# Projecting two of three row chunks first, normalising them beside the third, and leaving the meta rows out after the merge

## What is computed

```python
def _merge(x, o_a, o_b, rb, ga, gb, gla_norm_g, w_pa, w_pb, w_o, g, b):
    ...
    mixed = jax.nn.sigmoid(ga) * y_a + jax.nn.sigmoid(gb) * y_b
    return _layer_norm(ALPHA * x + mixed @ w_o, g, b)

def _ffn(x, w_gate, w_up, w_down, g, b):
    hdn = jax.nn.silu(x @ w_gate) * (x @ w_up)
    return _layer_norm(ALPHA * x + hdn @ w_down, g, b)
```

## Time and profile before

| what | value |
|---|---|
| median of 3 runs | 1925.07 us |
| the profiled execution: its own time, and its span | 1928.97 us, 1927.3 us |
| PE busy, share of the span | 1826.3 us, 95% |
| DVE, ACT, POOL busy | 724.2, 379.4, 475.2 us |
| mean granted TensorE clock | 0.962 |
| merge loop | 711.8 to 987.9 us |
| output projection | 992.4 to 1087.2 us |
| first FFN matmul, first `w_down` matmul | 1122.4, 1178.0 us |
| FFN groups but the last end | 1821.7 us |

### The profile page before, as it was taken

The page is one execution under the profiler, slowest core; times in us unless marked ns, Lnnn a source line. Parts: engine busy times, 40 slices in busy tenths (PEclk is TensorE's granted clock), DMA queues, the critical chain, the costliest instruction groups (busy, mean ns, idle before and its releaser), DMA issues.

```text
span 1927.3 us, 29265 instructions
## 1 busy us (share of the span) xinstructions
PE 1826.3 (95%) x11360; PEld 1654.4 (86%) x11360; DVE 724.2 (38%) x1303; ACT 379.4 (20%) x706; POOL 475.2 (25%) x283
## 2 busy tenths in 40 slices
PE   6999999998989899999999869999999999999994
PEld 5966666665768879999999769999999999999993
DVE  3156767541326352211156643123213313312318
ACT  3132232221312332011110260100100110010032
POOL 3310110110111203322232113322233232332225
PEclk8999999998987979999999989999999999999997
DMA  5134444303551111111111001111111111111102
GB/s 158 47 106 123 117 118 143 95 12 110 171 136 43 36 24 44 44 45 53 44 33 55 23 22 44 45 53 44 44 44 44 44 54 44 39 48 52 46 23 88
DMA packets 166780, 123.19 MB, mean 64 GB/s; under 512 B 22074, under 2 KB 140234, under 8 KB 166706
## 3 DMA queue, kind: packets, MB, share of 16 engines
q1 hardware_dynamic: 163154, 120.94, 21.6%
q10 hardware_dynamic: 3552, 1.25, 0.3%
HBM read 112.31 MB, written 9.85 MB: 63 GB/s over the span
## 4 chain that ended last, share of the span: by engine, by line
PE 88%; DVE 5%; ACT 2%; issue 2%; DMA 1%; SPq 1%; POOL 0%; POOLq 0%; ACTq 0%; DVEq 0%
PE psum L729 16%; PE psum L732 16%; PE psum L733 16%; PE psum L807 4%; PE psum L813 4%; PE psum L811 4%; PE psum L1256 4%; PE psum L1251 4%; PE psum L1255 4%; PE psum L962 4%; PE psum L935 2%; PE psum L938 1%; PE psum L891 1%; PE psum L1012 1%; PE psum L1192 1%
## 5 line engine op out<-in xcount | busy, mean ns | idle before, releaser
L729 PE MATMUL psum<-xh,wh 128*128 128x352 f32 (+1 forms) x1560 | 506.9, 325 | 20.3 <-DVE xl L2236 15.3
L732 PE MATMUL psum<-xl,wh 128*128 128x352 f32 (+1 forms) x1560 | 505.6, 324 | 0.0
L733 PE MATMUL psum<-xh,wl 128*128 128x352 f32 (+1 forms) x1560 | 504.6, 323 | 0.0
L677 POOL CAST wh<-raw 128x1024 fp32r<-128x1024 f32 x126 | 134.1, 1065 | 1406.2 <-PE psum L729 481.6
L729 PEld LDWEIGHTS psum<-xh,wh 128*128 128x128 f32 x1560 | 295.8, 190 | 22.1 <-issue 21.9
L679 POOL TENSOR_TENSOR wl<-raw,wh 128x1024 fp32r<-128x1024 f32 x126 | 310.7, 2466 | 10.1
L732 PEld LDWEIGHTS psum<-xl,wh 128*128 128x128 f32 x1560 | 295.7, 190 | 0.2
L733 PEld LDWEIGHTS psum<-xh,wl 128*128 128x128 f32 x1560 | 295.7, 190 | 0.0
L2261 DVE TENSOR_TENSOR hf<-sg,psum 128x352 f32<-128x352 f32 (+1 forms) x66 | 34.2, 518 | 412.8 <-PE psum L733 403.0
L807 PE MATMUL psum<-xh,wh 128*128 128x352 f32 (+1 forms) x480 | 164.4, 342 | 1.1 <-DVE negc_tok L1786 1.1
L811 PE MATMUL psum<-xl,wh 128*128 128x352 f32 (+1 forms) x480 | 161.4, 336 | 0.0
(11 more groups left out here) (293 smaller groups left out, 2350.0 us busy)
## 6 DMA issues: line engine op xcount, KB each, us to landing
raw<-in_w_in SPq DMA_DIRECT2D x86, 256.0 KB, 3.3
parts<-in_cache_k SPq DMA_DIRECT2D x64, 256.0 KB, 3.0
parts<-in_cache_v SPq DMA_DIRECT2D x64, 256.0 KB, 2.9
raw<-in_w_gate SPq DMA_DIRECT2D x44, 256.0 KB, 3.1
raw<-in_w_up SPq DMA_DIRECT2D x44, 256.0 KB, 3.2
raw<-in_w_down SPq DMA_DIRECT2D x44, 256.0 KB, 2.6
cb<-negc_scratch SPq DMA_DIRECT2D x8, 520.0 KB, 5.1
raw<-in_w_o SPq DMA_DIRECT2D x16, 256.0 KB, 3.1
```

What stands on the lines that cost most here:

```text
L677: pool.tensor_copy(wh[:, s, :], raw[:, r, :]).then_inc(sem("panel_high"), 1)
L729: first = mm(out, w[0], x[0], start=(n == 0), stop=False)
L732: mm(out, w[0], x[1], start=False, stop=False)
L733: last = mm(out, w[1], x[0], start=False, stop=(n == len(ks) - 1))
```

## The change

From the merge on all loops run over `BODY`, three chunks of 344 columns that leave out the 16 meta rows. The output projection is made in 24 units in a new order: chunks 0 and 1 of all eight tiles first (two units a panel), then chunk 2, for which panels 6 and 7 are still there and panels 0 to 5 are loaded and split a second time. The mean and square sums of chunks 0 and 1 are placed between the units of chunk 2 (after units 15, 16, 18 and 20), and DVE's and ACT's lists interleave their LayerNorm with the residuals of chunk 2. The first FFN group runs its first three panels on chunks 0 and 1, with the sums of chunk 2 between, and then on chunk 2; it is taken out of the loop. The scaling by ALPHA moves from ACT into DVE's additions of the first group. `ysq` (squares of all chunks) now lies over `xl`, `yrst` over `ol`. All other parts are unchanged.

```diff
+BODY = [(META, 344), (META + 344, 344), (META + 688, 344)]
-PAN_FFN = PAN_O + 8
+PAN_FFN = PAN_O + 14
-MEAN_BANKS, SQ_BANKS = [6, 7, 6], [7, 6, 7]
+OUT_UNITS = [(n, n, c) for n in range(8) for c in range(2)] + [(6, 6, 2), (7, 7, 2)] \
+    + [(8 + m, m, 2) for m in range(6)]
+NORM_SUMS = [("mean", 0, 6), ("mean", 1, 7), ("square", 0, 6), ("square", 1, 7), ("mean", 2, 6), ("square", 2, 7)]
...
-            for m in range(8):
-                panel_free(PAN_O + m)
-                columns((PAN_O + m) % RING, IN["w_o"][0], P * m)
+            for n in range(14):
+                panel_free(PAN_O + n)
+                columns((PAN_O + n) % RING, IN["w_o"][0], P * (n % 8))
...
+            for x, (n, m, c) in enumerate(OUT_UNITS):
+                if c == 0 or n >= 8:
+                    pe.wait_ge(sem("panel_split"), PAN_O + n + 1)
+                fresh = (n, c) in ((0, 0), (0, 1), (6, 2))
+                if fresh:
+                    pe.wait_ge(sem("mixed_split"), 2 * c + 1)
+                unit((PAN_O + n) % RING, x % 6, c, (oh, ol), begins=(c == 0 and n < 7) or (c == 2 and n >= 7),
+                     half=(sem("mixed_split"), 2 * c + 2) if fresh else None)
+                if x in (15, 16, 18, 20):
+                    norm_sum((15, 16, 18, 20).index(x))
...
+            p = PAN_FFN
+            for q in range(3):
+                pe.wait_ge(sem("panel_split"), p + q + 1)
+                for c in range(2):
+                    if q == 0:
+                        pe.wait_ge(sem("x1_split"), 2 * c + 1)
+                    unit(q, (A3, B3)[q % 2][c], c, (xh, xl), begins=(q == 0 and c == 0),
+                         half=(sem("x1_split"), 2 * c + 2) if q == 0 else None)
+                    if (q, c) in ((0, 0), (1, 0)):
+                        norm_sum(4 + q)
+            pe.wait_ge(sem("x1_split"), 5)
+            for q in range(3):
+                unit(q, (A3, B3)[q % 2][2], 2, (xh, xl), begins=(q > 0),
+                     half=(sem("x1_split"), 6) if q == 0 else None)
+            job(p + 3, 0, B3, ALL8, X8, chunks=BODY)
+            down(0, p)
...
-            act.wait_ge(sem("x1_split"), 6)
-            for k in range(KT):
-                do(mixed[:, k, :], mixed[:, k, :], ACT.Copy, scale=ALPHA).then_inc(sem("y_scaled"), 1)
+            squares(0)
+            squares(1)
+            root(0)
+            affine(0)
+            root(1)
+            affine(1)
+            squares(2)
+            gate_act(0, 0)
+            gate_act(0, 1)
+            root(2)
+            affine(2)
+            gate_act(1, 0)
...
+            for x in range(16):
+                residual(x)
+            deviations(0)
+            residual(16)
+            deviations(1)
+            residual(17)
+            residual(18)
+            normalise(0)
+            residual(19)
+            residual(20)
+            lows(0, 0)
+            residual(21)
+            normalise(1)
+            lows(0, 1)
+            residual(22)
+            lows(1, 0)
+            residual(23)
+            deviations(2)
+            lows(1, 1)
+            normalise(2)
+            lows(2, 0)
+            lows(2, 1)
...
+                    read(b, ve.scalar_tensor_tensor(out=y, in0=y, scalar=ALPHA, in1=psum[:, b, 0:cw],
+                                                    op0=ALU.mult, op1=ALU.add))
```

More of the change, by code:

```diff
@@ L713, in settled, with job @@
                 pe.wait_ge(bank_free[b], B.before(b))
-            def job(p, slot, banks, ks, xs, release=True, before_chunk=None, half=None, after=None):
+            def job(p, slot, banks, ks, xs, release=True, before_chunk=None, half=None, after=None, chunks=CHUNKS):
                 if p is not None:
                     pe.wait_ge(sem("panel_split"), p + 1)
-                for c, (c0, cw) in enumerate(CHUNKS):
+                for c, (c0, cw) in enumerate(chunks):
                     b = banks[c]
@@ L1204, in _, with unit @@
+                job(None, 0, B3, [4, 5, 6, 7], ((oh, ol), [4, 5, 6, 7]), release=False, chunks=BODY)
                 B.end(KT)
[L1207 to L1217, removed]
+            def unit(slot, b, c, x, begins=False, half=None):
+                take(b)
+                c0, cw = BODY[c]
+                out = psum[:, b, 0:cw]
+                for k in range(8):
+                    first = mm(out, wt(wh, slot, k), x[0][:, k, c0:c0 + cw], start=(k == 0), stop=False)
+                    if begins and k == 0:
+                        first.then_inc(sem("panel_used"), 1)
+                    mm(out, wt(wh, slot, k), x[1][:, k, c0:c0 + cw], start=False, stop=False)
+                    last = mm(out, wt(wl, slot, k), x[0][:, k, c0:c0 + cw], start=False, stop=(k == 7))
+                    if half is not None and k == 3:
+                        pe.wait_ge(half[0], half[1])
+                give(b, last)
@@ L1218, in norm_sums, with norm_sum @@
+            def norm_sum(n):
+                kind, c, b = NORM_SUMS[n]
+                c0, cw = BODY[c]
+                take(b)
+                if kind == "mean":
+                    pe.wait_ge(sem("ln1_sum"), c + 1)
                     last = mm(psum[:, b, 0:cw], ones[:, :], ysum[:, c0:c0 + cw], start=True, stop=True)
[L1219 to L1222, removed]
+                else:
@@ new lines, in _, with deviations @@
+            parts_added = [0]
+            norm_bank, norm_count, counted = {}, {}, {6: B.before(6), 7: B.before(7)}
+            for kind, c, b in NORM_SUMS:
+                counted[b] += 1
+                norm_bank[kind, c], norm_count[kind, c] = b, counted[b]
+            def deviations(c):
+                c0, cw = BODY[c]
+                b = norm_bank["mean", c]
+                dve.wait_ge(bank_full[b], norm_count["mean", c])
+                for q in range(2):
+                    y = mixed[:, 4 * q:4 * q + 4, c0:c0 + cw]
+                    ve.scalar_tensor_tensor(out=y, in0=psum[:, b, 0:cw].unsqueeze(1).to_broadcast([P, 4, cw]),
+                                            scalar=-1.0 / D, in1=y, op0=ALU.mult, op1=ALU.add)\
+                        .then_inc(sem("ln1_dev"), 1)
+                dve.wait_ge(sem("ln1_dev"), 2 * c + 2)
+                dve.sem_inc(bank_free[b], 1)
@@ new lines, in normalise, with lows @@
+            def normalise(c):
+                c0, cw = BODY[c]
+                dve.wait_ge(bank_free[norm_bank["square", c]], norm_count["square", c])
+                r = yrst[:, c0:c0 + cw]
+                link(ve.reciprocal(r, r))
+                for q in range(2):
+                    y = mixed[:, 4 * q:4 * q + 4, c0:c0 + cw]
+                    ve.tensor_tensor(y, y, r.unsqueeze(1).to_broadcast([P, 4, cw]), ALU.mult)\
+                        .then_inc(sem("ln1_norm"), 1)
+            def lows(c, q):
+                c0, cw = BODY[c]
+                four = slice(4 * q, 4 * q + 4)
+                dve.wait_ge(sem("x1_high"), 2 * c + q + 1)
+                ve.tensor_tensor(xl[:, four, c0:c0 + cw], mixed[:, four, c0:c0 + cw],
+                                 f(xh[:, four, c0:c0 + cw]), ALU.subtract).then_inc(sem("x1_split"), 1)
@@ L2281, in _ @@
                     settled(b)
[L2282 removed]
+                B.end(FGROUPS - 2)
             for u in range(2):
```

267 lines of the change are left out of this document (118 added, 149 removed).

## The result

| | before, same chip | changed kernel |
|---|---|---|
| median of the runs | 1925.24 us (1924.32 to 1928.29) | 1893.38 us of 4 (1889.22 to 1895.63) |
| ratio, 95% interval | | 0.9825 [0.981, 0.984] |
| profiled execution: time, span | 1928.97, 1927.3 us | 1893.1, 1891.4 us |

The changed kernel is 31.9 us faster.

A forecast was written before the change was run, and what follows sets the result against it. PE bounds the kernel, with LayerNorm 1 exposed. LayerNorm's 28.1 us, less 14.4 of stalls and 2.9 of clock, plus 11.9 of width, gains 22.7 us: 1902 us on the scale of the 1925.07 us median, range 1890 to 1910.

The forecast's parts named there:

- Width: Merge, projection, FFN: 344-column chunks save 0.06 us per 24 matmuls, 0.14 per 48 in `w_down`; 11.9 us together.
- DVE's list without disturbance: From the end of unit 21 to chunk 1's last low, DVE still has 19.0 us of work; PE has 13.9.
- Exclusion: DVE instructions with both inputs in SBUF and POOL's splits shut each other out, adding 8.9 us to DVE's list.
- Stalls and clock together: Around LayerNorm 1 in the new order: PE stands 14.4 us, and half clock after the last wait costs 2.9 us.
- the three pieces: PE's 14.0 us stall on `xl` and the mean sum, expected as waits of about 5, 6 and 3 us.
- LayerNorm's cost before: First `w_o` to first `w_down` matmul, old kernel: 21.4 us of standing PE plus 6.7 at half clock, 28.1 us.
- Covered at nothing: Six `w_o` panels loaded and split twice, extra transfers and ACT's changed work are hidden, costing PE 0 us.
- Rival 1: POOL's splits fall between DVE's instructions, so exclusion misses the path: stalls 5.5, clock 2.5, time 1893 us; chance 0.14.
- Rival 2: LayerNorm of chunks 0 and 1 falls behind the third chunk, only the width is left: 1913 us; chance 0.09.
- Rival 3: Clock stays at 1.2 GHz from the first FFN unit to the first `w_down`: slower, 1942 us; chance 0.04.

The follow-up runs named there:

- e1b: Kernel before with 344-column chunks from the merge on, output projection included, in the old order: 21.7 us faster than the kernel before, ratio 0.9887.
- e1: Kernel before with 344-column chunks from the merge on, except PE's projection jobs, in the old order: 18.2 us faster than the kernel before, ratio 0.9906.
- e2: Changed kernel with the old chunks of 352, 352 and 344 columns, so the new order alone: 15.8 us faster than the kernel before, ratio 0.992.
- e6: Changed kernel with chunks of 336, 352 and 344 columns in place of three of 344: 32.6 us faster than the kernel before, one run.
- e3: Changed kernel with POOL splitting only 128 of 1024 columns of eight panels (output wrong): 37.5 us faster than the kernel before, ratio 0.9803.
- after_again: Changed kernel unaltered, run again beside e8 on the same chip: 36.6 us faster than the kernel before, ratio 0.9817.
- e8: e7 with chunk 2's mean sum one FFN unit later, lows ahead of residuals 22 and 23, one cast moved: 42.7 us faster than the kernel before, ratio 0.9787.
- e5: Changed kernel with chunk 1's last low ahead of chunk 2's deviations and its normalisation ahead of residual 21: 37.5 us faster than the kernel before, ratio 0.9804.
- e7: e5 with the casts of eight panels on ACT, POOL only subtracting: 39.7 us faster than the kernel before, ratio 0.9787.

## Why the prediction came near, and where it was off

The profiled executions differ by 35.9 us in span. 1.4 of that is where the merge begins (711.7 and 710.3 us); it begins at 707.4 to 712.4 us in these runs, whatever the kernel, so it is not the change's. The other 34.5 stand against a sum of 22.7. Of the 11.8 us between them 6.0 are the width (point 1) and the rest is the order (points 3 to 5); both came out larger than forecast, so neither hides the other.

1. **Width, the step that failed:** "I take 0.06, in the middle". It came from one group of mixed widths, 3.85 and 3.80 us a chunk. Measured are 45.97 - 45.13 = 0.84 us for eight narrowed chunks in a group, 0.105 each, partly because the 344 chunks gain too when none is of 352: 158 ns a matmul between wide ones, 156.7 among equals. In `w_down`, where they don't, the two chunks of a group gave 0.31 us for 0.28. Merge 4.85, stage 1.6 (3.2 in e1b), groups and tail 11.4 make 17.9 us, where 11.9 was counted, with an upper bound of 13.4. The rows held a hint: they gave 0.07 and 0.045 for the same step in width. e1, e2 and e6 show this term. The estimate from the Trainium skill (TensorE: Matmul & The Clock Gate, section "Wait — 56ns, not 53.3ns?") was 15.4 us, nearer than mine; for the 344-column matmul itself that rule gives 145.8 ns, and the trace has 156.7.
2. **DVE's list without disturbance:** 19.0 us forecast, 19.6 in e3, where the short splits still stretch it a little. Right, in the order given.
3. **Exclusion:** 8.9 us forecast (its terms add up to 8.8); 6.7 of stretched instructions in the changed kernel, its path 26.5 us against 27.9. Measured for forecast, in order of the list: residual 21 lost 1.2 for 2.4, the normalisation 3.0 for 1.1, the low 0.8 for 2.4, residual 22 1.6 for 2.9. The mechanism was right, its size 2.2 us too large, and e3 shows that it is on the path. The sum came nearer than its terms, by luck: three were too large and one too small.
4. **Stalls and clock together:** 14.4 + 2.9 = 17.3 us forecast; 8.76 of standing and 4.1 of half clock, 12.9, measured. The path less PE's work is 26.5 - 13.9 = 12.6, and the three pieces with the half clock are 8.24 + 4.1 = 12.3: for the matmuls between two waits it makes no difference to the end whether PE stands or runs at 1.2 GHz. after_again shows it, with less half clock and more standing. The wrong step is "after the last it costs half of 5 us, with the mean sum 2.9 us": the full clock came back 0.7 us before the third wait ended, so only the mean sum was left to pay, 0.7 us (1.50 for 0.82), since DVE's list waits for it. In other executions something is left: in e3 and e8 the clock stays at half 6.1 and 3.1 us beyond the wait for the last low of chunk 1.
5. **LayerNorm's cost before:** 28.1 us. The order gained 16.7 (e2), 5.9 over forecast. In e2's trace PE stands 8.72 us, and is busy through two half-clock stretches of 3.4 us, where a matmul takes 0.293 us for 0.160, so 3.1 lost: 11.8 us, where 17.3 were forecast. That is 5.5 of the 5.9.
6. **Covered at nothing:** right. The six panels split twice cost PE no wait, since POOL waited for PE and not PE for POOL.

Rival 1 gave the number, 1893, by chance: it had the exclusion off the path and the width at 11.9. With the width at 17.9 it would have been 1887, and e3, which is about that rival made real, took 1888.5. The forecast with that width, 1896, is 3 us from the changed kernel's median. Rival 2 did not happen: e1b shows what it would have been (stage 182.4, against 167.4). Rival 3 did not happen: the longest half-clock stretch lasted 13.7 us, and the first FFN group ran at full clock behind it.

## What to carry to other kernels

Price a narrower loop from a stretch in which all chunks have the same width: a chunk among wider ones can hide much of the gain. When a wait and the clock's halving that follows it lie on one chain, price the other engine's chain alone and take PE's work off; extra are only half clock behind the last wait and half clock in a PE instruction that the chain itself goes through. Before DVE and POOL are put side by side, look which of DVE's instructions have two SBUF inputs: reordering those only moved the loss (e5), and giving POOL's casts to an idle third engine took 2.1 of 8.7 us off it (e7). What took most of PE's waits away was that PE no longer asked so early for what stands behind the stretched instructions (e8, 3.05 us for 6.41), with 6.6 us of stretching still there.

## What the runs showed of the hardware

- Chunks of unequal width cost more than equal ones of the same sum: 336, 352 and 344 columns give a group of 68.05 us, three of 344 one of 67.83 (e6). The third chunk, at the same columns, takes 158.0 and 156.8 ns a matmul in the jobs; in `w_down` nothing of it shows.
- The same kernel's half-clock stretches fall at other times in another execution: one of 13.7 us, or two of 3.4 us, around the same waits, and 6.8 or 3.4 us behind the merge. That moved the stage by 1.4 us: 0.6 behind the merge, 0.7 in the one mean sum that the chain waits for. It set the grain below which an edit could not be read from the stage's length alone.
